# Queries, keys and values of a windowed-attention layer projected channel-major instead of token-major

## The reference, cut to what matters

```
q, k, v, z = split(x @ w_in, [1024, 1152, 1280])
q, k = rope(q), rope(k)
# rope on each head of 64: x1, x2 = the two halves of 32
#   [x1 * cos - x2 * sin, x2 * cos + x1 * sin]
s = (q . k) * 64 ** -0.5      # keys of the own and the previous block of 128, inside the window
p = softmax([s, sink])[..., :-1]
y = ((p . v) * silu(z)) @ w_out
x = layernorm(4 ** 0.25 * x + y)
```

## Time and profile before

| | |
|---|---|
| median of 3 runs | 985.26 us (984.84 to 986.24) |
| the profiled execution | 985.34 us |
| its span, first to last instruction | 983.5 us |
| TensorE busy | 957.8 us, 97% of the span |
| VectorE busy | 643.0 us, 65% |
| ScalarE busy | 452.1 us, 46% |
| mean granted clock of TensorE | 0.998 |

### The profile page before, as it was taken

How to read it: one execution, slowest core, us unless ns; L and a number is a source line. 1 busy time by engine, 2 the same in 40 slices (tenths; PEclk the granted TensorE clock), 3 DMA queues, 4 the chain that set the end, 5 groups by cost and what they waited for, 6 DMA issues and landing times.

```text
span 983.5 us, 19957 instructions
## 1 busy us (share of the span) xinstructions
PE 957.8 (97%) x7678; PEld 788.1 (80%) x7678; DVE 643.0 (65%) x1212; ACT 452.1 (46%) x1310; POOL 314.2 (32%) x635
## 2 busy tenths in 40 slices
PE   7999999999999899999999999999999999999997
PEld 6888788787878687888788888888787777778885
DVE  4576868676777768574546666753443677789575
ACT  5655557566666565664455211230213555556000
POOL 1008474755565564746100000010010535440000
PEclk9999999999999999999999999999999999999999
DMA  6233322414142415131301522130303201013211
GB/s 219 66 77 101 87 81 55 113 37 128 37 113 55 113 32 133 29 103 48 113 22 51 175 75 65 45 95 1 97 22 65 67 24 46 24 67 112 82 65 64
DMA packets 95181, 73.80 MB, mean 75 GB/s; under 512 B 32848, under 2 KB 84208, under 8 KB 95088
## 3 DMA queue, kind: packets, MB, share of 16 engines
q1 hardware_dynamic: 60768, 55.69, 19.2%
q10 hardware_dynamic: 34320, 16.84, 6.8%
HBM read 61.47 MB, written 11.04 MB: 74 GB/s over the span
## 4 chain that ended last, share of the span: by engine, by line
PE 82%; DVE 8%; ACT 6%; issue 2%; DMA 1%; POOL 0%; ACTq 0%; DVEq 0%; POOLq 0%
PE ps L800 28%; PE ps L989 15%; PE ps L1172 9%; PE ps L1061 9%; PE ps L1002 2%; DVE tok L1596 2%; PE ps L1194 2%; PE ps L1137 2%; PE ps L959 2%; DMA ws_raw<-in_b_w_in 1%; PE ps L970 1%; PE ps L968 1%; PE ps L877 1%; PE ps L947 1%; PE ps L946 1%
## 5 line engine op out<-in xcount | busy, mean ns | idle before, releaser
L800 PE MATMUL ps<-act_hi,w_hi 128*128 128x512 f32 x512 | 223.7, 437 | 0.1
L800 PE MATMUL ps<-act_hi,w_lo 128*128 128x512 f32 x512 | 201.1, 393 | 0.0
L800 PE MATMUL ps<-act_lo,w_hi 128*128 128x512 f32 x512 | 200.1, 391 | 0.0
L1596 DVE SCALAR_TENSOR_TENSOR tok<-xs,convw,tok 128x512 f32<-128x512 f32 x144 | 115.3, 801 | 15.5 <-ACT xs L1295 13.7
L713 POOL TENSOR_TENSOR rank<-inverse,tok 128x60 f32<-128x60 f32 (+24 forms) x248 | 94.3, 380 | 97.6 <-DMA tok<-blocks_in 79.4
L800 PEld LDWEIGHTS ps<-act_hi,w_lo 128*128 128x128 f32 x512 | 96.1, 188 | 21.3
L800 PEld LDWEIGHTS ps<-act_hi,w_hi 128*128 128x128 f32 x512 | 97.0, 189 | 12.0 <-issue 0.3
L716 POOL TENSOR_TENSOR inverse<-inverse,rank 128x60 f32<-128x60 f32 (+24 forms) x248 | 100.2, 404 | 19.4
L800 PEld LDWEIGHTS ps<-act_lo,w_hi 128*128 128x128 f32 x512 | 97.2, 190 | 10.1
L989 PE MATMUL ps<-wo_lo,act_hi 128*128 128x512 f32 x224 | 87.4, 390 | 0.1
L989 PE MATMUL ps<-wo_hi,act_hi 128*128 128x512 f32 x210 | 82.5, 393 | 0.2 <-DVE act_lo L1688 0.2
(11 more groups left out here) (268 smaller groups left out, 2088.1 us busy)
## 6 DMA issues: line engine op xcount, KB each, us to landing
w_raw<-in_a_w_in ACTq DMA_DIRECT2D x32, 512.0 KB, 4.2
tok<-in_x SPq DMA_DIRECT2D x8, 512.0 KB, 7.1
decay<-gc_rows SPq DMA_DIRECT2D x8, 512.0 KB, 5.0
tok<-blocks_in SPq DMA_DIRECT2D x32, 128.0 KB, 2.6
v_turn<-v_tok SPq DMA_DIRECT2D x8, 512.0 KB, 5.8
v_tok<-v_turn SPq DMA_DIRECT2D x32, 128.0 KB, 2.9
xres<-in_x SPq DMA_DIRECT2D x8, 512.0 KB, 3.4
ws_raw<-in_b_w_in SPq DMA_DIRECT2D x16, 256.0 KB, 2.7
```

The costliest lines, as they stand in the source:

```text
L800: mm = pe.matmul(ps[:, g % 2, :], lhs[:, k, :], rhs[:, k, HALF * b:HALF * (b + 1)], start=(i == 0), stop=(i == GROUP - 1))
L1596: ins = dve.scalar_tensor_tensor(conv[b], xs[:, b, k:k + HALF], convw[:, k, tile:tile + 1], conv[b], ALU.mult, ALU.add)
```

## The change

The queries, keys and values are projected as the gate is: the stationary operand is a tile of 128 output channels of the weights, the moving one 512 tokens of the activations, and the result has channels on partitions. There are 20 groups: `KV_GROUPS` are keys, values for tokens 0 to 511, then keys, values for tokens 512 to 1023, and 16 query groups of a channel tile and a token half follow. The banks are 2, 3, 6, 7 and then 5, 6, 7 in turn, so a query group waits for the rotation of the group three before.

The halves of a head now lie 32 partitions apart. ScalarE copies them exchanged into `swapped` (four instructions of 32 partitions by 512, `swap_halves`), and VectorE forms the product with the cosines from PSUM, the product of the copy with the sines, and the sum (`rotate`), which lands in `bT` or `kd` directly. Keys need six instructions on VectorE in halves of 64 partitions beside the product with the sines. The tables are turned by TensorE once (`turn_tables`, eight transposes) and copied by ScalarE and VectorE. The values come out with channels on partitions and are turned back (`turn_values`, twice four transposes). The interleaved pair is now groups 10 and 11. The logits of units 0 and 1 follow groups 14 and 16. The gather of `v_rows` waits for the last rotation. The small tiles of the softmax (`sm`) have another place in memory.

```diff
-TOKEN_BANKS = (0, 1, 6, 7)
+KV_GROUPS = 4
+QK_GROUPS = KV_GROUPS + 2 * NK
+ROPES = QK_GROUPS - 2
+GROUP_BANKS = [2, 3, 6, 7] + [5 + n % 3 for n in range(KV_GROUPS, QK_GROUPS)]
-GATE_FROM = 18
+GATE_FROM = 13
-EARLY_LOGITS = 20
+FIRST_LOGITS, FIRST_MAXIMA, FIRST_EXPONENTIALS = (14, 16), (15, 17), (16, 18)
+REFILL_AT = 10
...
+def slices_before(n):
+    if n < KV_GROUPS:
+        return (2 * n, 2 * n + 1)
+    if n == KV_GROUPS:
+        return (WR - 1,)
+    return range(WR, SLICES) if n == REFILL_AT else ()
...
-            sp.wait_ge(q_val, NT)
+            sp.wait_ge(q_val, 2)
...
-                    sp.wait_ge(q_group, 3 * NT)
+                    sp.wait_ge(q_rope, ROPES)
...
# project_step
+                    if n == 0:
+                        pe.wait_ge(L[0]["yev"], 2 * (NT - 1))
+                        pe.wait_ge(q_kvlo, 2)
+                        pe.wait_ge(L[0]["xlo"], NT)
+                    elif n == 2:
+                        pe.wait_ge(L[0]["xlo"], 2 * NT)
+                    elif n == KV_GROUPS:
+                        pe.wait_ge(q_rope, 2)
+                    elif n == KV_GROUPS + 1:
+                        pe.wait_ge(q_vch, 2)
+                    elif n >= KV_GROUPS + 3:
+                        pe.wait_ge(q_rope, rope_of(n - 3) + 1)
...
-                    lhs = (act_hi, act_hi, act_lo)[j]
-                    rhs = (hi, lo, hi)[j]
+                    lhs = (hi, hi, lo)[j]
+                    rhs = (act_hi, act_lo, act_hi)[j]
+                    mm = pe.matmul(bank, lhs, rhs[:, k, HALF * b:HALF * (b + 1)],
...
# end of out_stage(0) on TensorE
-                    project_tokens(0)
-                    project_tokens(1)
+                    project_channels(0)
                     turn(NT - 1)
+                    turn_tables()
+                    project_channels(1)
...
# ScalarE
+            def swap_halves(n):
+                r = rope_of(n)
+                act.wait_ge(q_group, n + 1)
+                if r >= 2:
+                    act.wait_ge(q_rope, r - 1)
+                for a in range(0, P, 32):
+                    b = a + 32 - 2 * (a % 64)
+                    ins = act.activation(other_half(r)[a:a + 32], ps[b:b + 32, GROUP_BANKS[n], :], ACT.Copy,
+                                         scale=SCALE if n >= KV_GROUPS else 1.0)
+                ins.then_inc(q_swap, 1)
+            for n in range(QK_GROUPS):
+                for m in slices_before(n):
+                    high_slice(m)
+                if n == GATE_FROM:
+                    high_gate(0)
+                if is_value(n):
...
+                else:
+                    swap_halves(n)
...
# VectorE, a query group of rotate(n)
+                    own.next(dve.scalar_tensor_tensor(bT[:, tile, cut], ps[:, GROUP_BANKS[n], :], SCALE, cosr[:, cut],
+                                                      ALU.mult, ALU.mult))
+                    own.next(dve.tensor_tensor(other, other, sinr[:, cut], ALU.mult))
+                    own.wait()
+                    dve.tensor_tensor(bT[:, tile, cut], bT[:, tile, cut], other, ALU.add).then_inc(q_rope, 1)
# a key group
+                    own.next(dve.tensor_tensor(other, other, sinr[:, cut], ALU.mult))
+                    for c in range(KVH):
+                        own.next(dve.tensor_tensor(kd[rows, c, keys], ps[rows, GROUP_BANKS[n], :], cosr[rows, cut],
+                                                   ALU.mult))
+                    own.wait()
+                    for c in range(KVH):
+                        own.next(dve.tensor_tensor(kd[rows, c, keys], kd[rows, c, keys], other[rows], ALU.add))
+                    own.wait()
+                    for c in range(KVH):
+                        ins = dve.tensor_copy(kd[64 - 64 * c:128 - 64 * c, c, keys], kd[64 * c:64 * c + 64, c, keys])
+                    ins.then_inc(q_rope, 1)
...
+            for n in range(QK_GROUPS):
+                for m in slices_before(n):
+                    low_slice(m)
+                if n == FIRST_MAXIMA[0]:
+                    dve.wait_ge(q_c, 17)
+                    biased(0)
+                elif n == FIRST_MAXIMA[1]:
+                    biased(1)
+                if not is_value(n):
+                    rotate(n)
```

More of the change, by code:

```diff
@@ L155, in last_tile, with is_value, rope_of, tile_of @@
     return i == 1 and t == NT - 1
-def slices_before(n, refill):
-    if n < 2:
+def slices_before(n):
+    if n < KV_GROUPS:
         return (2 * n, 2 * n + 1)
-    if n < WR - 2:
-        return (n + 2,)
-    return range(WR, SLICES) if n == refill else ()
+    if n == KV_GROUPS:
+        return (WR - 1,)
+    return range(WR, SLICES) if n == REFILL_AT else ()
+def is_value(n):
+    return n < KV_GROUPS and n % 2 == 1
+def rope_of(n):
+    return n // 2 if n < KV_GROUPS else n - 2
+def tile_of(n):
+    return (n - KV_GROUPS) // 2, n % 2
 def plan(at, lag):
@@ L321, in hybrid_trunk @@
         kv_lo = sbuf(stp, "kv_lo", [P, NK, 2 * P], F32R)
-        cosr = sbuf(stp, "cosr", [P, NT, HD])
-        sinr = sbuf(stp, "sinr", [P, NT, HD])
-        rot = sbuf(stp, "rot", [P, 2, HALF])
+        swapped = sbuf(stp, "swapped", [P, 2, HALF])
+        vv = sbuf(stp, "vv", [P, NT, P])
         stp.close()
+        taken[0] = after_projection
+        late = ExitStack()
+        swapped_late = [None] * 2
+        for i in range(2):
+            sbuf(late, f"beside_late{i}", [P, (WR - 2 + i) * HALF])
+            swapped_late[i] = sbuf(late, f"swapped_late{i}", [P, HALF])
+        late.close()
         taken[0] = after_projection
@@ L341, in hybrid_trunk @@
         z_lo[0] = sbuf(stz, "z_lo0", [P, NK, P], F32R)
+        sm = {n: sbuf(stz, "sm_" + n, [P, 2, 2, 4]) for n in ("neg", "sum", "rden")}
         room2 = sbuf(stz, "room2", [P, (spare_at - taken[0]) // 4])
@@ L1040, in project_step @@
             def project_step(n, k):
[L1042 to L1045, removed]
+                bank = ps[:, GROUP_BANKS[n], :]
+                if n < KV_GROUPS:
+                    b = n // 2
+                    cols = slice(P * (n % 2), P * (n % 2 + 1))
+                    hi, lo = kv_hi[:, k, cols], kv_lo[:, k, cols]
+                else:
+                    tile, b = tile_of(n)
+                    sl = (NK * (tile // 4) + k) % WR
+                    cols = slice(P * (tile % 4), P * (tile % 4 + 1))
+                    hi, lo = ws_hi[:, sl, cols], ws_lo[:, sl, cols]
@@ L1062, in project_step, with turn_tables, project_channels @@
                                    start=(k == 0 and j == 0), stop=(k == NK - 1 and j == PASSES - 1))
                 return mm
-            def project_tokens(n):
+            def turn_tables():
+                pe.wait_ge(q_small, 48)
+                pe.wait_ge(L[0]["yev"], 2 * NT)
+                for t in range(NT):
+                    mm = pe.transpose(ps[:, t // 4, (t % 4) * P:(t % 4 + 1) * P], vv[:, t, :], ident[:, :])
+                mm.then_inc(q_ttr, 1)
+            def project_channels(n):
@@ L1140, in logits @@
                 mm.then_inc(s_s, 1)
-            last = 2 * NT - 1
-            for n in range(2, 3 * NT):
+            last = KV_GROUPS + NK - 1
+            for n in range(2, QK_GROUPS):
                 if n == last - 1:
@@ L1199, in values @@
                 mm.then_inc(s_pv, 1)
[L1201 to L1207, removed]
+            for third in range(3):
+                project_gate(0, third)
+            pe.wait_ge(q_rope, ROPES)
             logits(2)
             logits(3)
-            pe.wait_ge(q_tev, 3 * NT)
             for k in range(PAIRS - 1):
@@ new lines, in _ @@
+            dve.wait_ge(q_ttr, 1)
+            for b in range(2):
+                for e in range(2):
+                    ins = dve.tensor_copy(sinr[64 * e:64 * e + 64, HALF * b:HALF * (b + 1)], ps[64:128, b, :])
+            ins.then_inc(q_sin, 1)
+            dve.wait_ge(q_cos, 1)
+            dve.wait_ge(q_sin, 1)
+            for n in range(QK_GROUPS):
[8 more added lines that the diff above has]
+                    rotate(n)
```

152 lines of the change are left out of this document (64 added, 88 removed).

## The result

The changed kernel takes 995.13 us (median of 4 runs, 994.5 to 996.22), the kernel before 985.05 beside it (4 runs, 984.68 to 986.24): a ratio of 1.0094, interval 1.0081 to 1.0107. It is slower by 10 us. The forecast was 983.4, with a range of 979.5 to 986.5: wrong in sign and outside the range.

The account below looks back on a forecast made before the run. TensorE was taken as the bound, nearly solid in the projection stretch. Work change -11.0, waits +2.6, +4.1 and +2.8, rate -0.7 gave -2.2; the clock walk's -1.85 was used: 983.4 us, range 979.5 to 986.5.

Parts of the forecast that it names:

- What is removed and added, and the rate: TensorE's projection: token turns go, a few transposes come, matmuls run at 0.231 us; -11.4 us in all.
- Wait 1: TensorE before query group 0 (group 4) waits for both key rotations: 2.6 us, 3.7 with slow copies.
- upper bound: TensorE's wait before group 4 if VectorE's copies within SBUF take 0.69 us each instead of 0.42: 3.7 us.
- Wait 2: At the weight refill, TensorE waits at group 12's last slice and before group 13: 4.1 us in all.
- the ring of raw buffers: Two raw buffers for weight slices (load, high part, low part, next load) set the refill's pace, not the matmuls.
- T: Start of the interleaved groups 10 and 11 at the refill; high slice 15 was forecast at T + 15.9 to 16.7.
- Wait 3: Before the first values, TensorE waits for the v_rows gather, now triggered 4.0 us later: 2.8 us.
- landing 0.5: Allowance of 0.5 us in the main forecast's range for when the v_rows gather lands.
- Rival B: Loads quicker, no wait for v_rows, refill and rate at low ends: 979.7 us, chance 0.18.
- rival D: TensorE's clock drops to half rate after the idle stretch before group 4, costing 5.6 us more: 989, chance 0.12.
- deciding point: Idle time on TensorE beyond which the clock was said to drop: over 3.2 us, read at the span's end.

Follow-up runs that it names:

- e8: Changed kernel with six banks for the query groups, the gather in two halves and VectorE's new order of low slices: 976.45 us, ratio 0.9902 to the kernel before.
- e4: Changed kernel with one ScalarE copy of 128 partitions for four of 32, halves not exchanged, so not a correct rotation: 983.91 us, ratio 0.9969 to the kernel before.
- e3: Changed kernel with TensorE's four idle stretches filled by matmuls into a bank nobody reads: 989.61 us, ratio 1.0041 to the kernel before.
- e1: Changed kernel with the query groups on six banks in a hand-made order instead of three in turn: 986.98 us, ratio 1.0008 to the kernel before.
- e5: Changed kernel with six banks for the query groups and the gather in two halves: 977.84 us, ratio 0.9919 to the kernel before.

## Why the prediction was wrong

- **What is removed and added, and the rate** held: -11.95 for -11.4, and 12.0 read directly in e8. A step is 0.229 us, the lower end of the forecast's range, which took 0.231.
- **Wait 1** was the right wait with the right releaser, and its term was sized at half: 5.1 for 2.6. Two prices were carried from wide instructions to narrow ones: the start distance of two copies of 128 partitions (0.49) to copies of 32 (0.60), and a pair of 128-partition operations (1.28) to pairs of 64 partitions (1.41). Each is small, but they stand in series on one chain, three and two times. Three times 0.35 and two times 0.47 are 2.0 of the 2.5. e4 shows that the copies stand on the chain: with one in place of four, 3.1 us of the wait go. The upper bound that I gave (3.7) varied only the copies within SBUF, the one price that was right.
- **Wait 2**: 4.5 for 4.1. Reading the ring of raw buffers from the earlier trace rows was enough: high slice 15 came at T + 16.3 (693.62 to 709.90), forecast 15.9 to 16.7.
- **Wait 3**: 5.6 for 2.8. The trigger is 0.5 late, mostly by the same narrow copies; the gather lasted 1.9 to 2.0 longer, for which "landing 0.5" was far too little. That the sum took the gather's length from a single landing was its weak step: over the traces here it is 9.8 to 12.0. Rival B, quicker loads, went the wrong way.
- **The clock (rival D)** is the largest miss: the sum put it at nothing behind all three waits. I gave it 0.12, at one place, with a deciding point of over 3.2 us of idle and 5.6 of cost. The mechanism was right; the deciding point was read from a single place, the end of the span, and is wrong: a wait of 2.78 with another of 1.72 just before it, and in e4 one of 2.01, had a fallen clock behind them. I also treated it as an accident of wait 1, while my own sum had three waits of its kind. The price per fall is 1.7 to 2.4 in this trace, less than I said, but it came three times: 6.5 us, of which e3 gets 4 to 5.5 back in the time and 6.3 at its place.
- So of the 11.6 us between forecast and span, the clock is 6.5, wait 1 2.5, wait 3 2.8, wait 2 0.4, and the removed work -0.55. The clock alone did not turn the sign: with the measured waits and no clock the table still gives +3.3, and e3, which is that kernel, is slower than before (1.0041). e4, whose waits (2.0, 0.95 and 3.65) are in sum 2.9 us less than the forecast's 9.5, came out at 983.9 with the clock falling all the same; with the waits of the forecast and their clock the change would lie between even and slightly slower, which is argued and was not run.

The change itself is sound: TensorE's work shrinks by 12 us. What it lacked were banks and an order to go with the longer rotation. With six banks, the gather in halves and VectorE's order, 976.5 us are reached, 1% below the kernel before and 18 us below the change as it was made.

## What to carry to other kernels

When an edit lengthens the chain behind a product and takes buffers from it, add up that chain by instructions of the same width, to the end, and give the next user enough banks to cover it. Where TensorE was solid, price each new wait with the lower clock that may follow (here 1.7 to 2.4 us behind each of three), and not only the longest. A transfer that was just hidden isn't when its trigger moves; split, so that the first user waits for its own part alone, it was hidden again, and that gained 4.5 to 6 us in the time and 7.2 at its place.

## What the runs showed of the hardware

- The granted clock fell to 0.50 in or right behind idle stretches of 5.1, 5.5, 3.9 (e1), 3.7 (e4), 2.8 (with 1.7 shortly before) and 2.0 us (e4), and not behind those of 1.6 to 1.9 in the traced runs of e1 and e5. It came back 3 to 7 us after it fell. One fall cost 1.7 to 2.4 us in the first trace of the changed kernel, and over all traces from 1.5 (e1) to 3.0 (e4), both at the values.
- Filling the idle time with matmuls that nobody reads kept it at 1.00 and gained 4 to 5.5 us (e3).
- ScalarE's copies from PSUM of 32 or 64 partitions by 512, each at other partitions than the one before, start every 0.60 us, those of 128 partitions every 0.47 to 0.49: the narrow ones are not only no cheaper, they cost a quarter more. Why stays open.
- The last part of the 2 MB gather in four DMAs landed 9.8 to 12.0 us after its issue, over seven traces.
- VectorE's fp32 copies within SBUF, 64x512, took 0.43 us; its additions and products of the same size 0.70.
- Matmuls with 512 tokens moving start every 0.229 us; those of the earlier trace rows with channels moving 0.233.
